# A prefill-and-decode step: selected branch and prompt attention in one block, key and value rings laid out anew, sliding values loaded earlier

## The chip, the cores and the metric

The kernel runs on one core of one Trainium2 chip, in fp32 throughout. The metric is the device time of one launch in microseconds. All times below are counted from the start of the profiled span.

## The reference, cut to what matters

One layer of a hybrid decoder for one prompt of 1024 tokens and 8 samples of 4 new tokens each (8192 tokens of past). The part that matters here is mixer B of the samples, native sparse attention, and what follows it, the attention of the prompt:

```python
# samples, per (sample b, token t, KV head g); 4 query heads r share a KV head
p_slc   = sum over r of softmax(q . kc + bias)         # compressed branch, 128 blocks
top_i   = top 16 blocks of 64 tokens                   # first, current and previous block forced
o_slc   = softmax(q . K[blocks] + bias) @ V[blocks]    # paged cache_slc_k / cache_slc_v
o_win   = softmax(q . Kwin + bias) @ Vwin              # cache_win_k / cache_win_v, 512 + 4 keys
o_b     = g0 * o_cmp + g1 * o_slc + g2 * o_win
# mixer A: dilated attention, window groups (128,1), (512,4), (2048,16), for samples and prompt
# prompt: dilated (A), selected (all started blocks) and sliding branch, 1024 x 1024, causal
x = x + concat(o_a, o_b) @ w_out;  ConvFFN;  final norm
```

In the kernel the selected branch of a sample is computed over all 8192 keys, with a penalty added to the keys of blocks that were not chosen, so the whole key and value cache of that branch is read: 8 samples x 4 chunks, each chunk 128 x 2048 floats (1.05 MB), for keys and again for values, 64 gathers in all.

## The kernel before, in words

The program is a row of blocks; in a block each engine has its own instruction list, written by hand, and engines meet only at semaphores. Leaving a block, and clearing a stage's semaphores (`Mem.end`, L60), makes all engines wait for each other. The stages, with where they lie in the profiled span:

- `front` (input projection, compression) and `compressed_and_dilated` (L1222 ff.), one shared block, to about 620 us. In its last part PE works through the dilated window of the samples in 16 items (`Selected.turns`, `load_item`), each of about 1.8 MB, in 7 slots of 4096 columns of the large tile `space`. Keys of the second four samples are transposed until 593 us, then the values of that group are multiplied (`values(1)`, L1533) until 616.5 us, which gives `d_pv` its second count. SP loads the sliding keys (`cache_win_k`, two DMAs of 1 MB) as soon as the last keys are transposed, and then stores the compressed part of the prompt's mix in eight pieces of 256 KB (`scr_mixc`, L1454, semaphore `s_mixc`). POOL issues the first four key gathers (`gather_keys`) at 594 to 599 us.
- `sample_selected` (L1894 ff.), its own block, about 620 to 817 us. A ring of six half slots holds key chunks (`key(i)` is half slot 4 + i) and another six hold value chunks (`value(i)`: half slots 0 to 3, then 10 and 11). Half slots 8 and 9 first hold the sliding keys, and 10 and 11 the sliding values, which SP loads as the first thing of this block (L2041). PE: `window_keys` (L2111), `new_scores`, `window_scores`, then for each sample b and chunk c `keys(b,c)` (16 transposes of 128x128, L2175) and one chunk later `scores` (L2186); at (0,2) `window_probs`, at (0,3) `window_values` (L2164), which waits for the sliding values; for b >= 1 at c = 2 `probs(b-1)` (L2196), at c = 3 `values(b-1)` (L2214). PSUM has three banks for transposes; a bank is free when ACT or DVE has copied it (`by_act` says which of the two). DVE does both sliding softmaxes (L2352 to L2359) at (0,0), after its copies of chunk (0,0) and before those of (0,1). `scores(0,0)` waits until both are done with the score banks (`s_wl` 4). DVE's first `logits(0,0)` (L2370) waits for all eight `mixc` stores, because its buffer lies where they are read from.
- POOL issues all gathers of the stage. A key gather n waits until chunk n - 6 has been transposed. A value gather n waits from n = 4 on for `window_values` and from n = 6 on until PE has multiplied the values of sample (n - 6) // 4. They stand in one list, so what waits holds up all behind it.
- After the merge of the three branches (`merge`, L2225 to L2238, and DVE L2440 to L2448) comes `prompt_attention` (L909 ff.) in a block of its own, about 820 to 1164 us: 96 units of 128 queries, each with scores into PSUM (L1012), bias and maximum by DVE (L1167), exponentials by ACT (L1139), transposes (L1033) and values (L1053). The first item's operands are loaded during the stage before; POOL reverses the order of its queries at the start of the block (L1083, L1084).
- `ffn` (output projection, ConvFFN), to the end.

The DMAs that SP issues form one queue (q1 in the profile), those of POOL another (q0), and both use the same 16 DMA engines.

## Time and profile before

| what | us |
|---|---|
| three runs | 2131.23, 2125.96, 2129.39; median 2129.39 |
| the profiled execution, its own time | 2128.97 |
| its span, first to last instruction | 2126.8 |
| PE busy | 2033.3 (96%), granted clock 0.987 |
| DVE, ACT, POOL busy | 1116.7, 524.2, 571.3 |

The page divides the span in 40 slices of 53 us, each digit the busy share in tenths:

```profile
PE   6999999999878987999999999999999999999998
...
PEclk8999999999998999999999999999999999999999
DMA  8467677663796995232252315555666522601100
```

A 9 means nine tenths or more. Slices 11 to 15 (585 to 850 us by the place in the row, counting from 0) are those in which PE is below nine tenths and the DMA engines above it: these are the end of the dilated stage, the selected stage and the start of the prompt.

### The profile page before, as it was taken

What the parts mean: (1) busy time and instruction counts of PE and PEld (TensorE: products, weight loads), DVE (VectorE), ACT (ScalarE), POOL (GpSimd) and SP (SyncE); (2) the same over time, 40 slices, a digit from 0 to 9 for tenths busy, and PEclk for the clock granted to TensorE, in tenths of its full rate; (3) what the DMA queues carried; (4) which work ended last, traced back from release to release, by engine and by line L of the source; (5) the groups of instructions that cost most, each with busy time, mean ns of one, the idle gap of its engine ahead of it and who ended that gap; (6) DMA issues with size and microseconds to landing.
All of it is one profiled execution on the core that took longest, in us unless ns stands there. A gap on an engine that the chain in (4) does not pass through costs nothing. (4 is left out here: it accounts for less than half of the span.)

```text
span 2126.8 us, 31772 instructions
## 1 busy us (share of the span) xinstructions
PE 2033.3 (96%) x12334; PEld 1330.5 (63%) x12334; DVE 1116.7 (53%) x2518; ACT 524.2 (25%) x1146; POOL 571.3 (27%) x746
## 2 busy tenths in 40 slices
PE   6999999999878987999999999999999999999998
PEld 3445466665555665666676447888888888644443
DVE  4034455411534555766676456777777755611452
ACT  4111010001323444766766011011111111000001
POOL 0443234202033641112223241332223222303110
PEclk8999999999998999999999999999999999999999
DMA  8467677663796995232252315555666522601100
GB/s 218 140 214 278 256 285 279 240 213 115 258 381 248 420 418 180 100 90 60 69 157 58 118 59 198 198 198 198 212 224 219 178 80 61 238 4 30 42 40 40
DMA packets 156392, 373.04 MB, mean 175 GB/s; under 512 B 36981, under 2 KB 95085, under 8 KB 138189
## 3 DMA queue, kind: packets, MB, share of 16 engines
q1 hardware_dynamic: 126420, 149.63, 22.2%
q0 software_dynamic: 25280, 149.44, 18.1%
q10 hardware_dynamic: 4544, 71.95, 9.6%
q8 instruction: 99, 1.62, 0.3%
q14 instruction: 49, 0.40, 0.1%
HBM read 343.68 MB, written 98.60 MB: 208 GB/s over the span
## 5 line engine op out<-in xcount | busy, mean ns | idle before, releaser
L2899 PE MATMUL ff_ps<-ff_hx,whole_aw 128*128 128x264 f32 x2464 | 550.5, 386 | 0.9 <-DVE ff_hx L3278 0.9
L2899 PEld LDWEIGHTS ff_ps<-ff_hx,whole_aw 128*128 128x128 f32 x2464 | 467.1, 190 | 80.8 <-issue 1.4
L805 DVE STREAM_TRANSPOSE whole_space<-whole_space 128x512 f32<-128x512 f32 x256 | 155.3, 674 | 153.4 <-PE joint_bank L614 153.4
L578 PE MATMUL joint_bank<-in_w,in_xT 128*128 128x512 f32 (+1 forms) x512 | 201.5, 547 | 0.0
L1167 DVE CUSTOM_DVE_ANT_0 pa_L<-pa_psS,whole_space 128x512 f32<-128x512 f32 (+3 forms) x288 | 141.1, 532 | 46.6 <-PE pa_psS L1012 45.6
L1139 ACT ACTIVATE pa_L<-pa_L,pa_nm 128x640 f32<-128x640 f32 (+3 forms) x192 | 142.0, 741 | 51.3 <-DVE pa_nm L1179 51.2
L578 PEld LDWEIGHTS joint_bank<-in_w,in_xT 128*128 128x128 f32 x512 | 95.0, 190 | 94.2 <-issue 87.6
L2925 PE MATMUL ff_ps<-ff_hx,whole_space 128*128 128x512 f32 x336 | 148.0, 593 | 0.0
L703 ACT ACTIVATE in_yout<-joint_bank 128x128 f32<-128x128 f32 (+5 forms) x88 | 41.0, 479 | 378.8 <-PE joint_bank L578 200.0
L3359 DVE SCALAR_TENSOR_TENSOR whole_space<-whole_space,ff_kept 128x1024 f32<-128x1024 f32 x88 | 124.4, 1414 | 3.1
L614 PE MATMUL joint_bank<-whole_space 128*64 128x256 f32 (+1 forms) x1152 | 121.6, 364 | 0.0
L1033 PE MATMUL pa_psT<-whole_ident,pa_L 128*128 128x128 f32 x816 | 112.9, 281 | 8.4 <-ACT pa_PT L1133 8.4
L1012 PE MATMUL pa_psS<-whole_space,pa_qT 64*128 64x512 f32 (+3 forms) x576 | 115.6, 507 | 5.5 <-POOL pa_qT L1083 5.5
L1033 PEld LDWEIGHTS pa_psT<-whole_ident,pa_L 128*128 128x128 f32 x816 | 87.2, 141 | 48.9 <-ACT pa_L L1139 17.9
L592 PE MATMUL joint_bank<-in_xT,in_w 128*128 128x352 f32 x384 | 117.6, 463 | 0.0
L3140 ACT ACTIVATE whole_space<-whole_space 128x1056 f32<-128x1056 f32 x22 | 23.8, 1083 | 368.5 <-DVE whole_space L3361 368.5
L2925 PEld LDWEIGHTS ff_ps<-ff_hx,whole_space 128*128 128x128 f32 x336 | 63.6, 190 | 80.6 <-issue 80.6
L1053 PE MATMUL pa_psO<-pa_PT,whole_space 128*64 128x128 f32 x1632 | 110.3, 279 | 0.9 <-DVE pa_tmp L1209 0.5
L1133 ACT ACTIVATE pa_PT<-pa_psT 128x512 f32<-128x512 f32 (+2 forms) x182 | 91.5, 538 | 56.2 <-PE pa_psT L1033 55.2
L614 PEld LDWEIGHTS joint_bank<-whole_space 128*64 128x64 f32 x1152 | 74.8, 137 | 47.2 <-issue 13.0
L2800 PE MATMUL ff_ps<-whole_space 128*128 128x512 f32 x224 | 97.7, 593 | 1.7 <-issue 1.7
L592 PEld LDWEIGHTS joint_bank<-in_xT,in_w 128*128 128x128 f32 x384 | 71.8, 190 | 42.3 <-issue 3.9
(435 smaller groups left out, 2647.8 us busy)
## 6 DMA issues: line engine op xcount, KB each, us to landing
out_new_a_k_s<-in_cache_a_k ACTq DMA_DIRECT2D x8, 4088.0 KB
out_new_a_v_s<-in_cache_a_v ACTq DMA_DIRECT2D x8, 4088.0 KB
whole_aw<-in_w_up SPq DMA_DIRECT2D x44, 512.0 KB, 7.6
in_w<-in_w_in SPq DMA_DIRECT2D x5, 2048.0 KB, 13.3
whole_space<-in_cache_a_k SPq DMA_DIRECT2D x8, 1024.0 KB
whole_space<-in_cache_a_v SPq DMA_DIRECT2D x8, 1024.0 KB
ff_hx<-in_w_down SPq DMA_DIRECT2D x14, 512.0 KB, 4.3
whole_space<-in_x_prompt SPq DMA_DIRECT2D x12, 512.0 KB, 9.2
```

Of the source, the lines that this page charges most:

```text
L578: mm = pe.matmul(ps[0:n, b, 0:width], xT[:, k, t * P:t * P + n], w[:, at % WBUF, k, 0:width], start=(k == 0), stop=(k == KC - 1))
L592: mm = pe.matmul(ps[:, b, 0:n], w[:, at % WBUF, k, c * P:c * P + P], xT[:, k, r0:r0 + n], start=(k == 0), stop=(k == KC - 1))
L614: mm = pe.matmul(psH[dh * HD:dh * HD + HD, r % 2, o0:o0 + n], w1[:, kv, t16, dh, :], rows[:, dh, t, :], start=(t16 == 0), stop=(t16 == 15) ...
L805: last = dve.transpose(put[:, dh, :, k * HD:k * HD + HD].rearrange("p t (g b) -> p t g b", g=2), got[:, :, :, dh, :])
L1012: pe.matmul(psS[:, c % 2, h, 0:w], qT[r, i, qt * P:qt * P + P], kT[i][r, j0 * P + k0:j0 * P + k0 + w], start=True, stop=True).then_inc(s_q ...
L1033: mm = pe.transpose(psT[:, b % 3, (x - x0) * P:(x - x0) * P + P], turned, ident[:, :])
L1053: mm = pe.matmul(psO[h * HD:h * HD + HD, u % 2, 0:P], V[i][:, j0 + j, v0:v0 + HD], PT[:, u % 3, (2 * j + h) * P:(2 * j + h) * P + P], star ...
L1139: nc.scalar.activation(x, x, ACT.Exp, bias=nm[:, s, h:h + 1], scale=1.0, accum_out=sm[:, s, h:h + 1]).then_inc(s_ex, 1)
L1167: dve.tensor_tensor_reduce(L[:, u % 3, h, 512 * x:512 * x + n], psS[:, c % 2, h, 0:n], T[it % 2][:, h, SEQ - w + 512 * x:SEQ - w + 512 * x ...
L2899: mm = pe.matmul(ps[:, bank_of(x, j, g), 0:H2], aw[:, j % 2, at, k, :], hx[:, bt, k, g * H2:g * H2 + H2], start=(k == 0), stop=(k == KH - 1))
L2925: mm = pe.matmul(ps[:, b, :], a[:, k, :], wd(k0 + k)[:, c0:c0 + 512], start=(k == 0), stop=(k == KD - 1))
L3359: dve.scalar_tensor_tensor(out=out[:, 0:SEQ], in0=U[:, v, k:k + SEQ], scalar=tap(k), in1=out[:, 0:SEQ], op0=ALU.mult, op1=ALU.add)
```

## The change

It does the following.

1. `sample_selected` and `prompt_attention` share one block, one set of eight PSUM banks and one set of semaphores (`late`). Each engine goes from its last instruction of the one to its first of the other. In place of the barrier stand waits on `s_merged` (the merge's own step counter): PE's second unit waits for step 7, SP's loads for the prompt's second item for step 10. POOL reverses the first item's queries at the end of its list for the selected stage, into a place of their own (`q0`), in two halves. The merge's products move from score banks 0 and 1 to 2 and 3. DVE waits for one more store (`s_mixed` 16) before the merge's last steps.
2. Rings: `key(i)` is now half slot 4, 5, 10, 11, 8, 9 and `value(i)` 0, 1, 2, 3, 6, 7. Half slots 6 and 7 are free with the last dilated keys, so SP loads the sliding values right behind the sliding keys, in the dilated stage, ahead of the `mixc` stores. Half slots 10 and 11 are free only with the last dilated values, so of the first four key gathers the first two stay where they were and the other two wait for `d_pv` 2.
3. `by_act`: of chunk (0,1) ACT copies pieces 0, 1 and 2 and DVE piece 3; before it was the other way round. `scores(0,0)` waits for the first sliding softmax only (`s_wl` 2), and `scores(0,2)` for both.

The diff, cut to its core:

```diff
     def key(self, i):
-        return self.half(4 + i)
+        return self.half((4, 5, 10, 11, 8, 9)[i])
     def value(self, i):
-        return self.half(i if i < 4 else 6 + i)
+        return self.half((0, 1, 2, 3, 6, 7)[i])
+    def load_window(self, sp, name, at, sem):
+        for x in range(2):
+            sp.dma_start(at(4 + x).rearrange("p (b t) c -> p b t c", b=4),
+                         self.io[name][4 * x:4 * x + 4, :, :].rearrange("b (p t) c -> p b t c", t=4)).then_inc(sem, 16)
...
+        self.q0 = at(slot[1] + 3 * SEQ + 4 * NB * NT, SEQ)
...
# compressed_and_dilated, POOL
             pool.wait_ge(d_pv, 1)
-            for c in range(4):
+            for c in range(2):
+                pre.gather_keys(pool, 0, c)
+            pool.wait_ge(d_pv, 2)
+            for c in range(2, 4):
                 pre.gather_keys(pool, 0, c)
# compressed_and_dilated, SP
             sp.wait_ge(d_tr, use["keys", NB - 1, NTL - 1] + 1)
-            for x in range(2):
-                sp.dma_start(pre.key(4 + x)..., io["cache_win_k"]...).then_inc(pre.s_wk, 16)
+            pre.load_window(sp, "cache_win_k", pre.key, pre.s_wk)
+            pre.load_window(sp, "cache_win_v", pre.value, pre.s_wv)
             for n in range(QT):
# sample_selected
-        psT = m.ps("psT", [P, 3, 512])
-        psS = m.ps("psS", [P, 4, 512])
-        psV = m.ps("psV", [P, 4, P])
+        psT = bank[:, 0:3, :]
+        psS = bank[:, 4:8, :]
+        psV = bank[:, 3, :].rearrange("p (a n) -> p a n", a=4)
-        block = m.block()
...
             if kind == "keys":
-                return at[2] == 3 if at[1] == 1 else at[2] % 2 == 0
+                if at[1] == 1:
+                    return (at[2] == 3) == (at[0] > 0)
+                return at[2] % 2 == 0
...
         def _(sp):
-            for x in range(2):
-                sp.dma_start(pre.value(4 + x)..., io["cache_win_v"]...).then_inc(s_wv, 16)
# sample_selected, end of POOL's list
+            pool.wait_ge(ops.s_q0, 16)
+            half = SEQ // 2
+            for x in range(2):
+                pool.tensor_copy(ops.q0[:, x * half:x * half + half].rearrange("p (t n) -> p t n", n=P),
+                                 backwards(ops.qL[0][:, x * half:x * half + half], half // P)).then_inc(ops.s_qr, 1)
# sample_selected, PE
-                if n == 0:
-                    pe.wait_ge(s_wl, 4)
+                if n in (0, 2):
+                    pe.wait_ge(s_wl, n + 2)
# sample_selected, DVE's merge
             dve.wait_ge(s_fp, 2)
+            dve.wait_ge(ops.s_mixed, 16)
             for w in range(2):
-                r = dve.tensor_tensor(o1[:, w, :], psS[:, w, 0:NB * 32], GB[:, 1 + w, :], ALU.mult)
+                r = dve.tensor_tensor(o1[:, w, :], psS[:, 2 + w, 0:NB * 32], GB[:, 1 + w, :], ALU.mult)
# prompt_attention
+            sp.wait_ge(s_merged, 10)
             load(1)
...
+                        q = qT[r, i, qt * P:qt * P + P] if it else ops.q0[r, qt * P:qt * P + P]
...
                     if s == 1:
                         pe.wait_ge(s_qr, 2)
+                        pe.wait_ge(s_merged, 7)
...
-            pool.wait_ge(s_ld[0], 96)
-            pool.tensor_copy(qT[:, 0, 0:P]..., backwards(qL[0][:, 0:P])).then_inc(s_qr, 1)
-            pool.tensor_copy(qT[:, 0, P:SEQ]..., backwards(qL[0][:, P:SEQ], QT - 1)).then_inc(s_qr, 1)
```

## Rows read from the trace of the kernel before

**Rows 1.** The page: the chain that ended last, by line.

```profile
PE ff_ps L2899 25%; PE ff_ps L2925 11%; PE ff_ps L2978 2%; PE ff_ps L2800 1%; PE ff_ps L2935 0%; PE ff_ps L2909 0%; PE ff_ps L2867 0%; DVE ff_hx L3275 0%; DVE ff_hx L3277 0%; DVE ff_hx L3278 0%; DVE ff_hx L3266 0%; DVE ff_hx L3259 0%; PE ff_ps L2943 0%; ACT whole_space L3152 0%; DVE whole_space L3403 0%
```

**Rows 2.** Busy time by stretch: us (instructions), granted PE clock, DMA share, GB/s.

```profile
602.00:620.00 18.00, 12.48 (x270) 9.12 (x269) 2.63 (x7) 1.08 (x2) 0.00 (x0) 0.91 1.03 386
...
648.00:654.00 6.00, 0.27 (x8) 0.25 (x12) 0.74 (x4) 0.00 (x0) 0.00 (x0) 0.82 0.53 221
654.00:663.00 9.00, 9.00 (x104) 6.35 (x96) 1.98 (x4) 1.19 (x2) 3.14 (x3) 0.55 0.19 57
663.00:680.00 17.00, 16.20 (x230) 11.84 (x227) 9.67 (x22) 7.13 (x17) 3.23 (x4) 1.00 0.56 220
...
700.00:800.00 100.00, 88.29 (x1203) 63.12 (x1201) 54.72 (x115) 41.56 (x88) 55.85 (x54) 1.00 1.01 418
...
816.00:821.00 5.00, 0.05 (x2) 0.08 (x2) 1.20 (x4) 0.00 (x0) 0.48 (x2) 0.50 0.08 13
821.00:828.00 7.00, 7.00 (x30) 3.58 (x32) 4.19 (x20) 4.33 (x14) 1.26 (x3) 0.64 0.94 315
900.00:1000.00 100.00, 95.81 (x906) 67.40 (x902) 67.50 (x277) 69.42 (x161) 17.97 (x42) 1.00 0.26 72
```

**Rows 3.** Timeline of PE, 636 to 659: start, us, what, [idle before <- releaser].

```profile
636.42 1.12 PE L2175 MATMUL sb_psT<-whole_ident,whole_space 128*128 128x128 f32 x4 [4.33 <-DVE whole_space L2272]
637.47 1.93 PE L2186 MATMUL sb_psS<-whole_space,sample_Qb 128*32 128x512 f32 x8
639.33 3.08 PE L2175 MATMUL sb_psT<-whole_ident,whole_space 128*128 128x128 f32 x16
...
646.67 1.06 PE L2186 MATMUL sb_psS<-whole_space,sample_Qb 128*32 128x512 f32 x8
653.74 1.94 PE L2164 MATMUL sb_psV<-whole_space,sb_PTw 128*32 128x128 f32 x32 [6.00 <-DMA whole_space<-in_cache_win_v]
...
658.62 3.66 PE L2175 MATMUL sb_psT<-whole_ident,whole_space 128*128 128x128 f32 x16
```

**Rows 4.** Timeline of POOL: two value gathers that waited.

```profile
659.53 0.96 POOL L2069 DMA_INDIRECT whole_space<-in_cache_slc_v,sample_idx  x1 [14.05 <-PE sb_psV L2164]
...
680.11 0.95 POOL L2069 DMA_INDIRECT whole_space<-in_cache_slc_v,sample_idx  x1 [13.40 <-PE sb_psT L2175]
```

**Rows 5.** Timeline of PE, at 675.

```profile
675.28 3.68 PE L2214 MATMUL sb_psV<-whole_space,sb_PT 128*32 128x128 f32 x128
```

**Rows 6.** Timeline of SP's DMA issues; the first row is of 590 to 596.

```profile
593.19 1.73 SPq L1449 DMA_DIRECT2D whole_space<-in_cache_win_k  x2
595.96 9.70 SPq L1454 DMA_DIRECT2D scr_mixc<-cd_qp  x1
...
618.54 0.39 SPq L1458 DMA_DIRECT2D scr_mixT<-cd_mixA  x1
620.31 4.33 SPq L2041 DMA_DIRECT2D whole_space<-in_cache_win_v  x2
```

**Rows 7.** The gathers' DMA queue in 594 to 600: packets, MB, share of 16 engines.

```profile
q0 software_dynamic: 10, 0.08, 6.8%
```

**Rows 8.** The gathers' queue and SP's in 600 to 608.

```profile
q0 software_dynamic: 322, 2.38, 77.8%
q1 hardware_dynamic: 321, 0.64, 22.3%
```

**Rows 9.** SP's queue in 616 to 624.

```profile
q1 hardware_dynamic: 1871, 2.84, 99.0%
```

**Rows 10.** Timeline of all engines, 813 to 822.

```profile
813.44 1.97 PE L2238 MATMUL sb_psS<-sb_stackW,sample_vcs 128*128 128x32 f32 x16 [0.72 <-DVE sb_stackW L2436]
...
816.70 0.60 DVE L2448 TENSOR_TENSOR whole_space<-sample_mixB,sb_o 64x128 f32<-64x128 f32 x2
...
820.95 3.28 PE L1012 MATMUL pa_psS<-whole_space,pa_qT 64*128 64x128 f32 x12 [5.54 <-POOL pa_qT L1083]
...
821.90 0.29 DVE L1167 CUSTOM_DVE_ANT_0 pa_L<-pa_psS,whole_space 128x128 f32<-128x128 f32 x1 [4.60 <-PE pa_psS L1012]
```

More of the change, by code:

```diff
@@ L199, in __init__, with loaded @@
         self.s_mixc = m.sem("prompt_compressed_kept")
+        self.s_q0 = m.sem("first_queries_loaded")
+        self.s_qr = m.sem("queries_reversed")
+        self.q0 = at(slot[1] + 3 * SEQ + 4 * NB * NT, SEQ)
+    def loaded(self, it):
+        return self.s_ld[it % 2], 96 * (it // 2 + 1) - (0 if it % 2 else 16)
     def load_rows(self, sp, it):
@@ L906, in backwards, with prompt_attention @@
     return bass.AP(x.tensor, x.offset + step * (cols - 1), [[part, n], [step * cols, tiles], [-step, cols]])
-def prompt_attention(nc, io, scr, mixT, wo, cv, ident, ops, s_mix, s_wo, s_cvl):
+def prompt_attention(nc, io, scr, mixT, wo, cv, ident, ops, s_mix, s_wo, s_cvl, s_merged, late, bank, block):
     QT = SEQ // P
@@ L1889, in _, with sample_selected @@
                         dve.tensor_copy(outp[n], psX[:, 0, :]).then_inc(s_o[0], 1)
-def sample_selected(nc, io, scr, mixB, GB, Qb, idx, pre, ident, pen, OV, knew, s_nl, ops):
+def sample_selected(nc, io, scr, mixB, GB, Qb, idx, pre, ident, pen, OV, knew, s_nl, ops, late, bank, block):
     NQ = 4
@@ L1983, in sample_selected @@
         s_fp = m.sem("merge_step_by_pe")
-        block = m.block()
         use, on_act = {}, []
```

94 lines of the change are left out of this document (46 added, 48 removed).

## The prediction, made before the change was run

> **What bounds the kernel now.** I read the chain that ended last first, to know in which stages a saved microsecond comes through. As far back as it goes it is PE in the feed-forward part, matmul behind matmul [rows 1]; the prompt's attention before it has PE busy for 95.81 of 100 us and the DMA engines for a quarter (the row of 900) [rows 2]. Both are limited by their own PE work and load nothing that is tied to a point in time, so an earlier start of the prompt should reach the end whole. The question is when the prompt starts.
>
> The busy time by stretch then shows three kinds of time in the selected stage [rows 2]. In 700 to 800 the DMA engines are full (1.01, 418 GB/s): there the stage runs at the pace of its gathers. In 648 to 654 PE does 0.27 us of work in 6, and behind that hole the DMA engines are nearly empty too (0.19 in 654 to 663, 0.56 in 663 to 680). And in 816 to 821 PE and DMA both stand. The timelines say why. PE waits 4.33 us before 636.42 for copies by DVE, and 6.00 us before 653.74 for the sliding values [rows 3]. POOL's value gather of 659.53 waited for the product of those values (14.05 us), and that of 680.11 for the product of the first sample's values (13.40 us), which PE makes from 675.28 to 679.2 [rows 4, 5]. So the early PE holes empty the DMA queue, and from the gather of 680.11 on the queue stays full. The whole later stage hangs on when that gather goes out.
>
> **The change part by part.** I work against the profiled execution, 2128.97 us, 0.4 us under the median of the three runs.
>
> *Who copies chunk (0,1), and the split wait.* DVE copies the three pieces only after both sliding softmaxes, and PE stands 4.33 us for the first of them. With ACT copying pieces 0 to 2 (its list has nothing else there) PE transposes the fourth piece, computes `scores(0,0)`, which needs only the first softmax, and transposes half of chunk (0,2), until its bank waits for DVE's one copy, which ends about when PE goes on now, at 636.4. That is 1.12 + 1.93 + 1.54 (half of 3.08) = 4.6 us of work [rows 3] moved into the hole. DVE saves two copies, ACT takes two more. `scores(0,2)` then ends near 643.1 in place of 647.73 (646.67 + 1.06): gain **4.6**, between 3 and 5.
>
> *Sliding values loaded 25 us earlier.* Before, the issue stands at 620.31 and takes 4.33 us [rows 6]. After, it stands behind that of the sliding keys (593.19). The 6.00 us wait goes, if the values are there by 643, which the queue sums below give (about 619). Gain **6.0**. What is late next is not the keys of sample 1: their gathers (chunks 4 to 8) go out as before, in a queue of unchanged bytes.
>
> *PE's clock behind the hole.* In 654 to 663 PE is busy all the time at a granted clock of 0.55, close to the lower of its two levels (1.2 GHz), after it had stood still for 6 us; 16 transposes take 3.66 us there [rows 2, 3]. In the same 9 us at the full level I would expect up to 4 us less, and nothing less if the hole that remains (about 2 us at 634 to 636) is enough to hold it down. The nearest row is that of 663 to 680, with short holes and clock 1.00. I take **3**, range 0 to 4.
>
> *What these are worth later.* All three bring forward the first sample's value product, hence `s_pv` 1, hence the gather of 680.11, and the stream behind it is continuous to the end of the stage. I count them at full value: 13.6. The DMA engines have room for it: in 648 to 680 they carried 0.53 x 6 + 0.19 x 9 + 0.56 x 17 = 14.4 us worth of 32 [rows 2], so 17.6 us of them were empty, more than the shift.
>
> *The two key gathers that now wait.* Chunks 2 and 3 are issued at 616.5 and not at 597 and 598. PE wants chunk 2 at about 634, and neither was waited for before. POOL has nothing else there, and needs twice 0.96 us [rows 4] and a little between, so it reaches the barrier at about 618.8, with SP (618.54 + 0.39 [rows 6]). Cost 0.
>
> *SP's queue at the barrier.* Sliding values (two DMAs of 1.05 MB) now stand before the eight `mixc` stores, the new values and the store of `mixA`, and SP must have issued all of these before the barrier. The issue of the first store already took 9.70 us at 595.96, held up by a full queue [rows 6]. Two more issues cost 1.73 us if the queue takes them, as those of the sliding keys did [rows 6]; on the other hand, from about 607 SP's queue has the engines for itself, for want of gathers 2 and 3. The bounds are 0 (SP is held up by the queue anyhow, which now drains faster) and 3 (the held-up issues stand one behind the other). I take **+1**.
>
> *The mixc stores.* DVE's `logits(0,0)` waits for them. When both queues have work, SP's gets 0.64 MB in 8 us and the gathers' 2.38 [rows 8], so 0.08 against 0.30 MB per us; alone SP's moves 2.84 MB in 8 us, 0.355 per us [rows 9], and both together 0.386 (the row of 602) [rows 2]. Behind the item loads SP's queue must carry the block choice 0.5, sliding keys 2.1, sliding values 2.1 and mixc 2.1: 6.8 MB, of which 0.2 by 607, when gathers 0 and 1 (2.1 MB) are through. The next gathers are issued at 616.5 but move nothing for about 5 us, as those of 594.3 moved 0.08 MB before 600 [rows 7]. From 607 to 621 SP's queue moves 14 x 0.355 = 5.0 MB, or 5.4 at 0.386 (sliding keys and values are through by about 619). The 1.6 or 1.2 MB left take until 641 or 636 at 0.08 per us. DVE wants them at 637.4. I take a delay of **+2**, range 0 to 5. Before, SP's queue had the engines to itself there [rows 9], and the stores were in time.
>
> *One block.* Before, DVE ends the merge at 816.70 + 0.60 = 817.30 and does the first logits of the prompt at 821.90; PE ends its merge at 815.41 and starts the prompt at 820.95 [rows 10]. After, PE's first unit follows at 815.5 (the queries were reversed behind POOL's last gathers, the rest of the operands is loaded), its second within a us, after step 7 of the merge, and DVE goes on at 817.3: gain 821.90 - 817.30 = **4.6**. Also, the clock is 0.50 in 816 to 821, and 0.64 in 821 to 828 where PE is busy for 7.00 of 7 us [rows 2]. With no pause the start of the prompt should lose less: at most 7 x 0.36 = 2.5, at least nothing, because DVE sets the pace of the first small units. I take **1.0**. The second item's loads go out behind DVE's first logits and not just ahead of them, some 3 us later in this count; they are wanted eight units on. Cost 0. DVE's new wait for `mixA`'s store is for something issued at 618.54 [rows 6]; PE's second unit and all of DVE's prompt work are queued behind it. Cost 0. Reversing the queries, 1 us of POOL, is hidden behind the last value gathers. The semaphores of two stages are now cleared together after the prompt: between 0 and 0.5 us, taken as 0.
>
> *Sum:* -4.6 - 6.0 - 3.0 + 1.0 + 2.0 - 4.6 - 1.0 = **-16.2**, so 2128.97 - 16.2 = 2112.8, and with the 0.4 to the median **2113**. The best ends give -5 - 6 - 4 + 0 + 0 - 4.6 - 2.5 = -22.1 (2107), the worst -3 - 6 - 0 + 3 + 5 - 4.6 - 0 + 0.5 = -5.1 (2124).
>
> **The rivals.**
>
> *The gathers are the bound all along.* If the stage is bound by its bytes, early gains only fill the queue earlier and are given back. For it: 1.01 over 100 us [rows 2], and two thirds of the stage look like that. Against it: the 17.6 us of empty engines. It would leave the boundary alone: 2129.4 - 5.6 = 2123.8. The Trainium skill (DMA: Bandwidth & Descriptors, Rules for kernel authors) speaks for this one: spreading transfers over issuing engines gains no bandwidth, because all run on the same 16 engines. The full row of 700 agrees with it, the rows of 648 to 680 show that bandwidth was not what lacked there.
>
> *The boundary does not close.* PE or DVE meets another wait there (bank, queries, operands), and only the early gains stay: 2129.4 - 10.6 = 2118.8.
>
> *SP's queue starves.* This one ends on the other side. If SP's queue goes into 621 with 2.6 MB left and not 1.2 to 1.6, because the held-up issues left it empty for about 3 us, or the gathers start to move at 618 and not at 621, then at 0.08 MB per us the mixc stores land only when the gathers have run dry, at about 653 to 655. DVE stands at `logits(0,0)` for 18 us, with it the copies of chunk (0,2), PE and every gather behind. The time is 2129.4 - 10.6 + 3 + 18 - 5.6 = 2134.2, with no gain of clock. It costs more than everything else brings from 16 us of delay on, which is from a landing at about 653. For it: the 4 to 1 sharing [rows 8], the 9.70 us issue [rows 6]. Against it: a full megabyte would have to be missing from a sum of 6.8.
>
> **How the numbers follow.** The forecast as summed, 0.78; bound by bytes, 0.08; boundary does not close, 0.08; starved queue, 0.04; something else on either side of no change, 0.02. The predicted time is that of the forecast. The range is 2105 to 2123: the forecast's bounds without the outermost us at the upper end, with 2 us more at the lower one, for a clock that helps more than counted; the boundary rival lies in it. A measurement of this kernel can tell about 0.3%, 6.4 us. Faster: the forecast save its worst end and the boundary rival, 0.86. Same: bound by bytes (5.6 us) and the worst end of the forecast, 0.10. Slower: 0.04.
>
> **What would show it.** In the changed kernel: the wait of L2164 for the sliding values is gone and the product starts near 644; the 4.33 us hole is 2 us or less; the clock of the 9 us behind is near 1.00 (if it is still near 0.55, that term is wrong); the second stalled value gather goes out near 669 and the merge ends near 806; between DVE's last merge step and the prompt's first logits there is under 0.5 us; the block ends about 16 us before 1164. If SP reaches the barrier after 622, or DVE waits for `mixc` longer than 5 us at L2370, the queue sum is wrong. If the gather of 680.11 moves forward by 12 us and the merge by less than 5, the first rival holds. The prediction is wrong altogether if a stage behind 821 runs longer than before.

## The result, and the profile after

The changed kernel takes 2130.53 us in the median of 22 runs, against 2127.78 for the kernel before: a ratio of 1.0014, 95% interval 1.0009 to 1.002. The interval lies just above 1, so the kernel is slower by a hair, and within the 0.3% that the prediction takes as no change. 2113.0 was forecast, with a range of 2105 to 2123. The profiled execution of after spans 2128.8 us, that of before 2126.8.

Busy time by stretch of after (us, then PE, PEld, DVE, ACT, POOL busy, PE clock, DMA share, GB/s), to be held against [rows 2]:

```profile
620.00:632.00 12.00, 0.70 (x4) 0.67 (x5) 0.60 (x2) 0.00 (x0) 0.24 (x2) 0.50 0.88 345
648.00:654.00 6.00, 6.00 (x36) 3.97 (x37) 4.62 (x10) 1.71 (x3) 5.25 (x5) 0.72 0.98 381
654.00:663.00 9.00, 8.54 (x129) 5.68 (x128) 5.63 (x16) 2.58 (x6) 3.67 (x4) 1.00 0.73 279
700.00:800.00 100.00, 89.43 (x1195) 62.84 (x1194) 53.94 (x117) 41.74 (x91) 56.11 (x55) 0.98 1.02 416
816.00:821.00 5.00, 5.00 (x22) 2.31 (x22) 2.87 (x13) 3.33 (x11) 0.59 (x2) 0.65 0.89 277
900.00:1000.00 100.00, 96.86 (x934) 68.39 (x932) 65.57 (x269) 68.03 (x162) 18.35 (x43) 1.00 0.26 73
1155.60:1162.80 7.20, 0.01 (x1) 0.02 (x1) 0.43 (x2) 0.00 (x0) 0.61 (x2) 0.63 0.00 0
1162.80:1175.50 12.70, 12.69 (x81) 5.13 (x81) 2.05 (x4) 1.20 (x2) 4.79 (x4) 0.63 0.90 328
```

The holes that the change was aimed at are gone: PE is busy for all of 648 to 654 (0.27 us before), the 9 us behind run at clock 1.00 (0.55 before), and 816 to 821 is full. But two stretches in which PE does nothing are new: 620 to 632, and 1155.6 to 1162.8.

The first one, in PE's timeline of after (start, us, what, [idle before <- releaser]), which answers to [rows 3]:

```profile
631.30 0.39 PE L2120 MATMUL late_bank<-whole_ident,sample_knew 32*128 32x32 f32 x2 [14.34 <-PEq L70]
...
647.22 1.37 PE L2190 MATMUL late_bank<-whole_ident,whole_space 128*128 128x128 f32 x8 [1.72 <-DVE whole_space L2287]
...
655.23 1.06 PE L2179 MATMUL late_bank<-whole_space,sb_PTw 128*32 128x128 f32 x32
...
657.93 2.00 PE L2190 MATMUL late_bank<-whole_ident,whole_space 128*128 128x128 f32 x16
```

The hole of 4.33 us is now 1.72, the product of the sliding values waits for nothing, and 16 transposes take 2.00 us where they took 3.66. All of it lies behind a pause of 14.34 us at the barrier (the sequencer, PEq, at L70). SP's issues and POOL's timeline, which answer to [rows 6] and [rows 4], say what held the barrier:

```profile
594.82 13.35 SPq L143 DMA_DIRECT2D whole_space<-in_cache_win_v  x2
608.21 9.06 SPq L1466 DMA_DIRECT2D scr_mixc<-cd_qp  x6
...
624.67 0.49 SPq L1470 DMA_DIRECT2D scr_mixT<-cd_mixA  x1
```

```profile
616.27 0.94 POOL L149 DMA_INDIRECT whole_space<-in_cache_slc_k,sample_idx  x1 [19.25 <-PE joint_bank L1545]
617.51 0.94 POOL L149 DMA_INDIRECT whole_space<-in_cache_slc_k,sample_idx  x1 [0.30 <-issue]
631.11 0.12 POOL L2092 MEMSET sb_Ln<- 128x32 f32 x1 [12.66 <-POOLq L70]
...
677.76 0.96 POOL L2079 DMA_INDIRECT whole_space<-in_cache_slc_v,sample_idx  x1 [11.76 <-PE late_bank L2190]
```

SP was through at 625.2 and not at 618.9, 6.2 us later. POOL (GpSimd) had issued its last gather by 618.45 and then stood for 12.66 us. The raw records of the trace name it: a DRAIN of GpSimd, an instruction with which the block ends. It lasts until 629.88; the last gathers landed at 624.6 and 627.7. The page counts no drain as work, it shows only as idle time "<-POOLq".

The boundary to the prompt closed as forecast [rows 10], and then the end of the merged block opened. DVE's first logits of after; the first FFN work of after on POOL and PE; and PE's of before:

```profile
814.14 0.29 DVE L1177 CUSTOM_DVE_ANT_0 pa_L<-late_bank,whole_space 128x128 f32<-128x128 f32 x1
```

```profile
1162.64 1.27 POOL L3050 TENSOR_TENSOR whole_space<-whole_space 128x512 f32<-128x512 f32 x1 [6.17 <-POOLq L70]
...
1162.81 1.08 PE L2804 MATMUL ff_ps<-whole_space 128*32 128x512 f32 x4 [7.20 <-PEq L70]
```

```profile
1164.68 0.64 PE L2787 MATMUL ff_ps<-whole_space 128*32 128x512 f32 x4 [1.90 <-PEq L70]
```

Again GpSimd's drain: 5.48 us from 1155.99, where before it took 0.56. The two spans come apart as follows (differences of start times in the two traces, us):

| stretch | before | after | change | forecast |
|---|---|---|---|---|
| start to POOL's first work behind the barrier | 620.31 | 631.11 | +10.80 | +1 |
| from there to the second stalled value gather | 59.80 | 46.65 | -13.15 | -13.6, +2 for mixc |
| from there to the end of the merge on DVE | 137.19 | 136.34 | -0.85 | 0 |
| boundary to the prompt's first logits | 4.60 | 0.04 | -4.56 | -4.6 |
| prompt attention, to PE's last product | 340.88 | 341.47 | +0.59 | -1.0 |
| gap before the FFN | 1.90 | 7.20 | +5.30 | 0 |
| FFN up to its first long group of products | 9.86 | 12.67 | +2.81 | 0 |
| that group (224 products) and all behind it | 952.26 | 953.32 | +1.06 | 0 |
| sum | 2126.8 | 2128.8 | +2.0 | -16.2 |

The second row counts from a barrier that stands 10.8 us later in after, and transfers went on in that time (the sliding values landed at 624.4, ahead of it). It shows that the waits behind the barrier are gone, and not what each change would be worth with the barrier in its old place.

### The profile page after: what moved, and what is told of

It is laid out like the page before. It is cut to its first block and busy times, and to the rows that moved or that the text cites. A ratio compares the mean times of both kernels' runs of the same rounds, so it can differ in the third digit from the quotient of the medians.

```text
span 2128.8 us, 31737 instructions
## 1 busy us (share of the span) xinstructions
PE 2035.3 (96%) x12334; PEld 1328.0 (62%) x12334; DVE 1105.1 (52%) x2516; ACT 525.4 (25%) x1148; POOL 577.0 (27%) x746
## 5 line engine op out<-in xcount | busy, mean ns | idle before, releaser
L1177 DVE CUSTOM_DVE_ANT_0 pa_L<-late_bank,whole_space 128x512 f32<-128x512 f32 (+3 forms) x288 | 141.1, 531 | 42.2 <-PE late_bank L1025 41.7
L1046 PE MATMUL late_bank<-whole_ident,pa_L 128*128 128x128 f32 x816 | 113.2, 281 | 8.5 <-ACT pa_PT L1143 8.5
L1046 PEld LDWEIGHTS late_bank<-whole_ident,pa_L 128*128 128x128 f32 x816 | 87.4, 141 | 49.7 <-ACT pa_L L1149 18.4
L1066 PE MATMUL late_bank<-pa_PT,whole_space 128*64 128x128 f32 x1632 | 110.3, 278 | 0.9 <-DVE pa_tmp L1219 0.5
L1143 ACT ACTIVATE pa_PT<-late_bank 128x512 f32<-128x512 f32 (+2 forms) x182 | 91.6, 539 | 56.7 <-PE late_bank L1046 55.3
L1025 PE MATMUL late_bank<-whole_space,pa_qT 64*128 64x512 f32 (+3 forms) x528 | 104.0, 498 | 0.0
```

Source lines behind the costliest of these rows:

```text
L1046: mm = pe.transpose(psT[:, b % 3, (x - x0) * P:(x - x0) * P + P], turned, ident[:, :])
L1066: mm = pe.matmul(psO[h * HD:h * HD + HD, u % 2, 0:P], V[i][:, j0 + j, v0:v0 + HD], PT[:, u % 3, (2 * j + h) * P:(2 * j + h) * P + P], star ...
L1177: dve.tensor_tensor_reduce(L[:, u % 3, h, 512 * x:512 * x + n], psS[:, c % 2, h, 0:n], T[it % 2][:, h, SEQ - w + 512 * x:SEQ - w + 512 * x ...
```

## The experiments

Two theories were set against each other first: that the two drains and what SP has queued took the gain back, or that the gain was never there (the gathers as the bound, the rings, the semaphores cleared together). Then each term of the sum was priced alone. Each median is of that kernel's runs, each ratio is to the kernel before on the same chip, with its 95% interval. The runs were made on several chips, on which the median of the kernel before lay between 2127.15 and 2129.18, so a difference between the medians of two rows is good to some 2 us; the ratios allow for the chip.

| run | base and edit | us | ratio |
|---|---|---|---|
| late_nodrain | after, merged block ends without the drain | 2121.15 | 0.9972 (0.9961 to 0.9983) |
| joint_nodrain | after, dilated block ends without it | 2125.37 | 0.9992 (0.9982 to 1.0002) |
| both_nodrain | both | 2118.31 | 0.9957 (0.9941 to 0.9972) |
| gathers_behind_barrier | after, key gathers 2, 3 behind the barrier | 2121.10 | 0.9963 (0.9949 to 0.9977) |
| behind_barrier_late_nodrain | that and late_nodrain | 2112.30 | 0.9937 (0.992 to 0.9955) |
| best_values_behind_barrier | that, sliding values behind the barrier | 2110.72 | 0.9928 (0.9907 to 0.9949) |
| best_unsplit | 2112.30's kernel without the split | 2117.33 | 0.9952 (0.9936 to 0.9968) |
| best_unmerged | 2112.30's kernel without the merge | 2116.42 | 0.9958 (0.9944 to 0.9972) |
| no_merge | after without the merge | 2126.92 | 1.0000 (0.9986 to 1.0013) |
| rings_alone | before with rings, early values, late gathers | 2130.79 | 1.0007 (0.9997 to 1.0017) |
| split_alone | before with the split | 2128.02 | 0.9999 (0.9989 to 1.0008) |
| before_gathers_behind | before, key gathers 2, 3 behind the barrier | 2118.69 | 0.9951 (0.9938 to 0.9964) |
| before_gathers_split | that and the split | 2115.15 | 0.9950 (0.9919 to 0.9981) |
| before_small_dma | before, one software DMA in the prompt's block | 2128.08 | 1.0008 (0.9995 to 1.0022) |

Three more have a single run each, for a drain's length: drain_in_the_middle, before_40_gathers, before_40_plain. The merge alone, on before's rings, was not measured: with a tile of its own for the reversed queries (merge_alone) the kernel's tiles do not fit into SBUF. So the merge is priced only on top of the rings.

### The drains

**late_nodrain.** GpSimd's drain at the end of the merged block is left out. Nothing here needs it for its data, as each gather is waited for by its reader.

```diff
-            block = late.block()
+            block = late.block(no_gpsimd_drain=True)
```

> After, with the merged block closed without GpSimd's drain. Theory (drains laid bare): in after the gap between the last product of prompt attention and the first of the FFN is 7.20 us (1155.61 to 1162.81), 5.48 of it GpSimd's drain, and the two groups of 32 products behind it take 6.02 us where before had 3.64. Without the drain the gap is 1.6 to 2.0 us, the groups take 3.6 to 4.2, and the time is 6 to 8 us under after's, 2122.5 to 2124.5. Rival (the merge costs by its semaphores): more are cleared at one place, so the gap stays at 6 us or more and the time within 1 us of after's. Rival (the gap is cover): output weights or FFN weights that load in it are late next, so the gap closes but the first products of the FFN wait as long, and the time falls by less than 2.

Measured: 2121.15, 9.4 us under after's median (8.9 by the ratios). The gap and the first products behind it:

```profile
1158.62 5.34 PE L2804 MATMUL ff_ps<-whole_space 128*32 128x512 f32 x32 [2.04 <-PEq L70]
```

The gap is 2.04 us, as expected, and the rival of the semaphores falls: the same are cleared at the same place (0.44 us in both). The 32 products still take 5.34 us, not 3.6 to 4.2; but from the first of them to the first long group it is 9.94 us (before 9.86, after 12.67). The long group itself takes 107.06 us (after 108.49, before 107.58). So the exposed drain cost 5.2 us itself, 2.7 by a colder start behind it (after's clock is 0.63 from 1155.6 through 1175.5, and 0.83 in late_nodrain over the same products) and up to 1.4 in the long group: 9.3 in these stretches. The two spans differ by 8.4, since PE came to the gap 1.0 us later here (1156.58 against 1155.61). My 6 to 8 left the last part out.

**joint_nodrain** and **both_nodrain.** The same edit to the block that ends in the dilated stage, and to both.

```diff
-                block = joint.block()
+                block = joint.block(no_gpsimd_drain=True)
```

> After, with the block that ends in the dilated stage closed without GpSimd's drain. Theory: there the drain waits for the two late key gathers (landed at 624.6 and 627.7, drain over at 629.88) while SP is free at 625.2; without it the barrier follows SP, at 626.2 to 626.8 instead of 631.11, and the 4.5 us stay to the end: 2125.5 to 2126.5. Rival (SP's queue alone holds the barrier): barrier at 631, time as after's 2130.5. Rival (the gathers bound the stage): the barrier comes earlier, but the value gathers still queue behind the same bytes, the window values product or the second stalled value gather starts where it did (655.2 and 677.8), and the time falls by under 1.5 us.

> After, with both blocks closed without GpSimd's drain. Theory: the two gains add, 10 to 12.5 us under after's 2130.5: 2118 to 2120.5, that is 7 to 10 us under before. Rivals: if either drain is cover for something else, the sum is short by that part (2123 to 2126).

Measured: 2125.37 and 2118.31, 5.2 and 12.2 us under after. In joint_nodrain the barrier follows SP, whose last issue came later than in after (626.14, not 624.67):

```profile
626.14 0.48 SPq L1470 DMA_DIRECT2D scr_mixT<-cd_mixA  x1
```

```profile
628.28 0.39 PE L2120 MATMUL late_bank<-whole_ident,sample_knew 32*128 32x32 f32 x2 [11.08 <-PEq L70]
```

The second stalled value gather moves with it, from 677.76 to 673.84, 3.9 us for 3.0 at the barrier: the stage is not held by its bytes. Without the drain the block does not wait for what is in flight: in both_nodrain PE starts behind the barrier at 624.73, and the last gather lands at 625.65. The theory of the drain holds, but it is half of the story, since PE still stands for 11.08 us.

And the first block's drain, left out, is not paid later. The drain at the end of joint_nodrain's merged block takes 5.47 us, as after's, though 294 software DMAs (DMAs that GpSimd issues) had gone out since the last one, and not 60. On POOL:

```profile
1161.19 2.50 POOL L3050 TENSOR_TENSOR whole_space<-whole_space 128x512 f32<-128x512 f32 x2 [6.18 <-POOLq L70]
```

**gathers_behind_barrier.** Both drains stay; key gathers 2 and 3 become POOL's first work behind the barrier.

```diff
             for c in range(2):
                 pre.gather_keys(pool, 0, c)
-            pool.wait_ge(d_pv, 2)
-            for c in range(2, 4):
-                pre.gather_keys(pool, 0, c)
...
+            for c in range(2, 4):
+                pre.gather_keys(pool, 0, c)
             pool.memset(Ln[:, :, :], NEG).then_inc(s_z, 1)
```

> After, with key gathers 2 and 3 issued first thing behind the barrier instead of ahead of it; both drains stay. Theory (the drain waits for gathers in flight): GpSimd's drain is over with gathers 0 and 1, by 613, the barrier follows SP at 624 to 627, and of the 4.5 to 6 us some 0 to 3 are lost to keys that land 10 us later: 2126 to 2129. Rival (SP's queue alone): the barrier stays at 629 or later and the time is after's or above, 2130.5 to 2133.

Measured: 2121.10, 9.4 us under after (10.9 by the ratios) and well below the 2126 to 2129 expected. SP and PE:

```profile
618.53 1.16 SPq L1467 DMA_DIRECT2D scr_mixT<-cd_mixA  x1
```

```profile
621.26 0.39 PE L2119 MATMUL late_bank<-whole_ident,sample_knew 32*128 32x32 f32 x2 [5.34 <-PEq L70]
```

Not only the drain is early (over by 609.58): SP's last issue ends at 619.7 and not at 625.2. I had taken SP's queue for delayed by the sliding values alone. The two gathers' bytes, the last of which landed at 627.7 in after, most often hold it up as well: in the seven profiles that have them ahead of the barrier together with the early sliding values, SP is through at 623.1 to 626.6 in six and at 617.2 in one (rings_alone); in the four that have only the early values there, at 617.9 to 619.7 in three and at 624.1 in one (best_unsplit). What makes the two exceptions is not shown. And nobody waits for the keys that come later: the second stalled value gather goes out 45.6 us behind the barrier's first PE work (46.5 in after). With the merged block's drain left out too (behind_barrier_late_nodrain, 2112 to 2116 expected) the time is 2112.30: the two losses add.

**drain_in_the_middle.** After with `pool.drain()` behind POOL's reversal of the first queries, where nobody waits for POOL.

> After, with one more drain of GpSimd behind its reversal of the first queries, while the other engines merge the branches; the drains at the blocks' ends stay. Theory (what the drain at the end clears is left by the software DMAs since the last drain, once): the added drain takes some 5 us where nothing waits for GpSimd, the one at the end under 0.8 instead of 5.48, the gap before the FFN is about 2 us, and the one look is some 5 to 8 us under after's. Rival (a drain at the end of a block with gathers has a fixed price): the last drain takes 5 us again and the time is after's.

One run: 2122.65. The added drain ran from 798.42 for 11.45 us, hidden, the one at the end of the block took 0.56, and the gap was 2.29 us:

```profile
1159.10 5.34 PE L2805 MATMUL ff_ps<-whole_space 128*32 128x512 f32 x32 [2.29 <-PEq L70]
```

So within a block a drain clears once what the software DMAs since the last one left. The added one was longer than the 5 us expected as it began ahead of the last landing (807.4).

**before_small_dma**, **before_40_gathers**, **before_40_plain.** What does the length go by? One plain software DMA at the start of the prompt's block, and 40 of either kind, one in each of its first 40 units, of 16 bytes a row:

```diff
             for s in range(U + 4):
+                if s < 40:
+                    pool.wait_ge(s_probe, 16 * s)
+                    pool.dma_start(probe[:, :], io["c_flip"][:, 0:4]).then_inc(s_probe, 16)
```

> Before, with one small software DMA (128 x 4 numbers) issued by GpSimd at the start of the block of prompt attention, landed some 300 us before the block ends; nothing else is changed. Theory (a block in which GpSimd has issued any software DMA pays a fixed drain): the drain at the end of the block grows from 0.56 us to about 5.5, the gap before the FFN from 1.90 to about 7, and with the colder clock behind it the time rises by 6 to 7.5 us, to 2134 to 2135.5. Rival (the drain costs by the number of software DMAs or their bytes, 36 gathers and more in after): the drain stays under 1.5 us and the time within 1.5 us of before's.

> Before, with 40 tiny gathers (indirect software DMAs, 128 rows of 16 bytes) issued by GpSimd in the block of prompt attention, one in each of its first 40 units. Theory (each gather leaves something that the next drain clears, 5.48 us for after's 60, 0.09 each): the drain at the end of the block takes 3 to 4.5 us where one plain software DMA left 0.66. Rival (bytes or large rows set it): under 1 us. The issues themselves may lengthen the units; only the drain is read here.

> Before, with 40 tiny plain software DMAs (128 x 4 numbers) issued by GpSimd in the block of prompt attention, one in each of its first 40 units, where before_40_gathers had gathers. Theory (every software DMA since the last drain leaves some 0.08 us for the next): the drain at the end of the block takes 3.5 to 4.6 us, as with 40 gathers (3.83). Rival (gathers alone leave something): under 1 us.

My theory of a fixed price fell with the first: its drain took 0.66 us and the time is before's. With 40 it took 3.83 us for gathers and 3.84 for plain ones. The issues themselves lengthened the units, to 2164.39 and 2144.78 in all. The drains of GpSimd at the ends of blocks, from the raw records:

| drain | software DMAs since the last drain | last landing | starts | lasts |
|---|---|---|---|---|
| before, prompt | 0 | | 1163.16 | 0.56 |
| before_small_dma, prompt | 1 | long before | 1163.57 | 0.66 |
| before_40_gathers, prompt | 40 | long before | 1194.75 | 3.83 |
| before_40_plain, prompt | 40 | long before | 1172.54 | 3.84 |
| after, merged block | 60 | 807.5 | 1155.99 | 5.48 |
| gathers_behind_barrier, merged block | 62 | long before | 1146.61 | 5.64 |
| joint_nodrain, merged block | 294 (60 of them in the block) | long before | 1154.53 | 5.47 |
| after and before, FFN | 0 | | 2044.01, 2042.15 | 3.28 |
| late_nodrain, both_nodrain, FFN | 60, 294 (none in the block) | long before | 2035.65, 2029.68 | 3.28 |
| before, selected | 60 | 810.4 | 801.41 | 11.44 |
| before, dilated | 234 | 616.3 | 595.80 | 22.66 |
| after, dilated | 234 | 627.7 | 616.61 | 13.27 |
| gathers_behind_barrier, dilated | 232 | 607.5 | 593.81 | 15.77 |

A drain's record opens before GpSimd's last instruction ahead of it is done, and its length holds what that one still needs. At the end of the prompt that is an addition of 0.45 us, over 0.07 us before the drain's end in before (1163.65 and 1163.72), and in the FFN one of 3.17 us, also over 0.07 before the end. In the rows of the dilated and the selected stage GpSimd's last gathers are still issued in it, in before's dilated one until 599.10 and in after's until 618.45. So the drain's own share of the 0.56 and of the 3.28 is near nothing.

Where all had landed, 0, 1, 40, 60 and 62 fit 0.56 us and 0.082 us for each: (3.84 - 0.56) / 40, and (5.48 - 0.56) / 60. Kind and size don't matter. Only those of the same block count: 234 of an earlier block add nothing in joint_nodrain (5.47 for 5.48), and 60 or 294 of earlier blocks add nothing to the FFN's 3.28. What takes them off where a block ends without the drain is not shown. Where some are still in flight, the drain ends 2.1 to 2.5 us behind the last landing. The price per DMA isn't shown beyond 62: 234 times 0.082 would be 19.2 us, and after's took 13.27.

### The terms of the sum, one by one

**no_merge** and **best_unmerged.** After without the merge, and the same with the gathers behind the barrier.

> After without the merge: before with the rings, the sliding values, the two late key gathers and the split of the first copies. Against after it tells what the merge is worth. Theory (4.6 us won at the boundary of prompt attention, 5.3 lost to the drain at the end of the merged block, up to 2 to a colder clock behind it): 1 to 3 us under after's 2130.5, so 2127.5 to 2129.5, with the barrier near 629 to 631 and a gap of 1.9 before the FFN. Rival (the merge is a gain, as the prediction had it): 4 us and more above after's, 2134.5 or later.

> The gathers behind the barrier, but no merge: no_merge with key gathers 2 and 3 behind the barrier; all drains are there, hidden behind the merge of branches or short. Against 2112.3 it prices the merge without its drain. Theory: the boundary is worth 4.6 us, so 2116 to 2118. Rival (most of the merge's gain was lost elsewhere in the prompt stage too, as after's 4.56 at the boundary but no more later): under 2114.

Measured: 2126.92 and 2116.42. With its drain in the open the merge costs 3.6 us (2130.53 - 2126.92; 3.0 by the ratios). Without that drain it gives 4.1 (2116.42 - 2112.30; 4.5 by the ratios). The intervals of the two ratios overlap in both cases. no_merge has the late barrier (PE starts at 631.19) and the short gap:

```profile
1163.01 3.64 PE L2794 MATMUL ff_ps<-whole_space 128*32 128x512 f32 x32 [1.89 <-PEq L70]
```

**split_alone** and **best_unsplit.** The split of the first copies alone in before, and taken out of the kernel of 2112.30.

```diff
-                return at[2] == 3 if at[1] == 1 else at[2] % 2 == 0
+                if at[1] == 1:
+                    return (at[2] == 3) == (at[0] > 0)
+                return at[2] % 2 == 0
...
-                if n == 0:
-                    pe.wait_ge(s_wl, 4)
+                if n in (0, 2):
+                    pe.wait_ge(s_wl, n + 2)
```

> The split of the first copies alone (which engine copies chunk 1 of sequence 0, and the wait in two steps) in before. Theory (the wait for the sliding values stands behind it): the hole of 4.33 us shrinks, and the products for the sliding values wait as much longer, since the values land at 653.7 all the same: 2127 to 2128.5, nothing gained. Rival (the prediction's terms add one by one): 4.6 us and part of the clock, 2120.5 to 2123.5.

> The fastest kernel so far (2112.3) with the first copies split as in before. It prices the hole of 4.33 us where nothing stands behind it. Theory (the prediction's terms of 4.6 and a part of the clock's 3.0): 2116 to 2119, with a hole of about 4 us back between 640 and 650. Rival (the products wait for keys there in any case, as these come later now): 2111 to 2113.5.

Alone it gives nothing, 2128.02. PE in split_alone:

```profile
636.42 1.38 PE L2177 MATMUL sb_psT<-whole_ident,whole_space 128*128 128x128 f32 x8 [0.85 <-DVE whole_space L2274]
...
654.34 1.93 PE L2166 MATMUL sb_psV<-whole_space,sb_PTw 128*32 128x128 f32 x32 [10.63 <-DMA whole_space<-in_cache_win_v]
```

The hole of 4.33 is 0.85, and the wait of 6.00 for the sliding values is 10.63: what one gave, the next wait took. Where no such wait stands behind it, the medians put the split at 5.0 us (2117.33 - 2112.30) and the ratios at 3.2, with intervals that overlap. The hole in best_unsplit and in the kernel of 2112.30:

```profile
641.62 0.82 PE L2187 MATMUL late_bank<-whole_ident,whole_space 128*128 128x128 f32 x4 [3.30 <-DVE whole_space L2284]
```

```profile
635.41 1.37 PE L2189 MATMUL late_bank<-whole_ident,whole_space 128*128 128x128 f32 x8 [1.05 <-DVE whole_space L2286]
```

Counted from the first PE work behind the barrier, as the profile of best_unsplit has a late barrier (625.66 against 619.46), the prompt's scores start 185.7 us later there and 181.2 in the other: 4.6. The same count, to the prompt's first logits, gives 3.3 for rings_alone and no_merge (191.83 and 188.49) and 2.7 for before_gathers_behind and before_gathers_split (193.04 and 190.33). So 3 to 5 us.

**rings_alone.** Before with the new rings, the early sliding values and the two late key gathers.

> The rings alone: before, with after's rings, sliding values and two late key gathers; no merge, and the first copies split as in before. Theory: the barrier slips by some 10 us as in after (GpSimd's drain behind the late gathers, SP's queue behind the sliding values), the wait for sliding values (6.0) goes and the hole of 4.33 stays: 3 to 5 us slower than before, 2131 to 2133, and a gap of 1.9 before the FFN. Rival (prediction: queues cost 3 at most): 2122 to 2125.

Measured: 2130.79, not told from before's time, at the lower edge of what the theory gave. SP's last issue, and PE:

```profile
616.27 0.93 SPq L1465 DMA_DIRECT2D scr_mixT<-cd_mixA  x1
```

```profile
630.27 0.39 PE L2109 MATMUL sb_psT<-whole_ident,sample_knew 32*128 32x32 f32 x2 [14.52 <-PEq L70]
```

Here SP is done at 617.2 and the barrier still comes 13 us later, by the drain alone.

**best_values_behind_barrier.** The sliding values go back behind the barrier in the kernel of 2112.30. Then **before_gathers_behind** and **before_gathers_split**: before, with no more than key gathers 2 and 3 moved behind the barrier, and with the split beside it.

```diff
-            for c in range(4):
+            for c in range(2):
                 pre.gather_keys(pool, 0, c)
...
+            for c in range(2, 4):
+                pre.gather_keys(pool, 0, c)
             pool.memset(Ln[:, :, :], NEG).then_inc(s_z, 1)
```

> The fastest kernel so far (gathers behind the barrier, no drain at the end of the merged block, 2112.3) with the sliding values loaded behind the barrier again, as before has them. It prices the early load where no drain hides it. Theory (the prediction's term of 6.0 holds): the values land at 645 to 652 instead of ahead of 630, the products wait 5 to 7 us at about 650, and the time is 2116.5 to 2120. Rival (the early load only moves bytes, since the key and value gathers then come sooner): 2111 to 2113.5.

> Before, with key gathers 2 and 3 moved from ahead of the barrier to the first place behind it; nothing else. Theory (the gathers, in large packets, hold up what SP has queued: the stores ahead of the barrier and the sliding values behind it): the barrier comes no later than 619, the sliding values land before 645 instead of at 653.7, their wait of 6.0 us goes, and the hole of 4.33 stays: 2119 to 2122.5. Rival (keys that come later are waited for, and the early load of the sliding values is what removes their wait): 2126 or more.

> The same with the first copies split as in after; still before's rings, no early load, no merge. Theory (the rings and the early load are worth nothing): as best_unmerged, which differs by them alone, 2115 to 2117.5. Rival (they are worth the prediction's 6.0): 2121 or more.

My first theory fell: 2110.72, and no wait for the sliding values, though they are issued at 618.61. The early load is worth nothing once the gathers are out of the way (the 1.6 us between the two medians are within their intervals). The second held: the two gathers alone, moved in before, give 2118.69, 9 us by the medians and 10 by the ratio, more than any term of the forecast, and a third of a us under the 2119 to 2122.5 expected. PE's hole stays, its wait for the sliding values is gone, as they land at 644.4 and not at 653.7:

```profile
636.29 1.11 PE L2177 MATMUL sb_psT<-whole_ident,whole_space 128*128 128x128 f32 x4 [4.44 <-DVE whole_space L2274]
```

The DMA queues in 600 to 612 show what changed (packets, MB, share of 16 engines), first before, then before_gathers_behind:

```profile
q0 software_dynamic: 473, 3.49, 76.7%
q1 hardware_dynamic: 471, 0.92, 21.6%
```

```profile
q1 hardware_dynamic: 869, 1.73, 47.8%
q0 software_dynamic: 288, 2.10, 51.8%
```

The gathers' 8 KB packets had left SP's 2 KB packets 0.92 MB in 12 us; with two gathers fewer SP moves 1.73. Its sliding keys and mixc stores are out of the way earlier, and the sliding values find a free queue: their two issues take 1.44 us together, not 4.33 [rows 6]. In before both queues move nearly the same number of packets while both have work, 473 and 471 here and 322 and 321 in [rows 8], so the one with 7.4 KB a packet (3.49 MB in 473) takes 3.8 times the bytes of the one with 2.0. The Trainium skill (DMA: Bandwidth & Descriptors, Queues, rings and completion order) says that each DMA engine takes turns between its queues packet by packet. Its packet is a group of typically 9 to 17 descriptors; the equal counts agree with such turns, but that its packets are the ones the profile counts is not shown. before_gathers_split comes out at 2115.15 (2115 to 2117.5 expected); the split's 3.5 us between these medians is not told from nothing by the ratios (0.9951 and 0.9950), and best_unmerged, which adds the rings and the early values, is no faster (2116.42).

## Why the prediction was wrong, point by point

**What bounds the kernel: right.** An earlier start of the prompt comes through to the FFN whole (-7.76 at the first logits, -7.17 at PE's last product of prompt attention), and the stream of gathers shifts with the gather of 680.11. The rival that the gathers are the bound is refuted by joint_nodrain. One loose statement ahead of the rows, on which no term rests: of the slices 11 to 15 the DMA engines are at nine tenths in 11, 13 and 14 alone, and PE is at nine tenths in 13.

**Who copies chunk (0,1): mechanism right, size about right.** 4.6 was taken; the hole fell from 4.33 to 1.72, and the split is worth 3 to 5 where nothing hides it. But it stood first in a chain of two waits, and alone it gives 0 (split_alone).

**Sliding values early: the wait went, the cause was wrong.** I took the wait of 6.00 for a matter of the issue time. It was one of the queue: the gathers ahead of the barrier held up what SP had to move. My own rows had it [rows 8], and I used them only for mixc. The values landed at 624.4 and not at about 619, in time all the same.

**PE's clock behind the hole: the clock right, its price not measured alone.** Clock 1.00 in place of 0.55, and 16 transposes in 2.00 us and not 3.66. With the two above, 13.15 of 13.6 us came, counted from the late barrier.

**The two key gathers later, cost 0: wrong, this is the step that failed.** I let POOL reach the barrier with the end of its last issue, at 618.8. It reached it at 629.9, since the drain waits for the landing (627.7) and 2.2 us more. The last gather's issue row of 0.94 us ends at 618.45, and the landing comes 9.3 us behind it. The Trainium skill (Perfetto Trace Analysis, DMA Instruction — SWDGE (GPSIMD)) says that such an instruction ends in the profile when its descriptors are made and not when the data has moved, and the landing times here agree. In before there was a drain too, over at 618.46 (last landing 616.3), half a us ahead of SP's 618.93, which hid it. What is hidden in the trace of before is not free when the work ahead of it moves by 19 us. The barrier came 10.8 us later and not 1, and with the two gathers behind it the kernel takes 9.4 us less.

**SP's queue at the barrier: +1, range 0 to 3, wrong.** It measured +6.2. In after the drain hides it, and with the drain left out the barrier follows it (joint_nodrain). Half of the premise failed: SP's queue did not have the engines for itself, as the bytes of the moved gathers came into it until 627.7. With them gone SP's last issue is over at 619.7. That the sliding values stand ahead costs little as a rule and 5 us in one profile (PE's first work behind the barrier, with the gathers behind it: 619.46, 620.07, 621.26 and 625.66 with them, 618.80, 620.33 and 621.85 without).

**The mixc stores: +2 did not come.** With the barrier at 631 they were in time (landed at 632.1, and DVE comes to its logits at 647.1), and with the gathers behind it also (624.4 and 635.3 in the kernel of 2112.30).

**One block: the boundary right (4.56 for 4.6), the drain missing, the second step that failed.** The merge took away the block end at which POOL's drain of 60 gathers was hidden (801.41 to 812.85, within the merge of branches), and put it where everyone waits: 5.48 us, and 2.8 more in a colder FFN start. I had priced the semaphores cleared together (0 to 0.5; 0.44 against 0.13 us), and not the drain beside them, which I put at nothing. The clock's 1.0 at the prompt's start did not come either: prompt attention took 0.59 us more, though 816 to 821 is full now, at clock 0.65.

**The rivals.** None was the one that came. The slower one (SP's queue starves, 2134.2) named the right queue, with the wrong waiter. The one that was missing: the barrier waits for what POOL has in flight.

**The sum.** -16.2 was forecast and +2.0 came, 18.2 us apart. The barrier is 9.8 of them (10.80 for 1), the gap and the cold start before the FFN 8.1 (5.30 and 2.81 for nothing); the rest, within 1.6 us a row, nearly cancels.

With both losses taken away the kernel runs at 2112.30 and 2110.72, beside the 2113 forecast. That is partly luck: of the terms, the early values' 6.0 is worth nothing in these kernels, and the gathers moved behind the barrier, which were no term, stand in its place.

## What to carry to other kernels

The end of a block makes GpSimd wait for the software DMAs in flight, and costs 0.08 us here for each that it issued in the block. Before moving a gather toward a block's end, or merging a block full of gathers with one behind it, look up in the records where the drain lies and what hides it; a drain set where GpSimd is idle, or left out where every reader waits for its data, brings the time back, and the one left out was not paid at the next block's end. A transfer that lands 25 us before its use should be looked at for what it delays: two gathers in large packets, moved behind a barrier, were worth 9 us here, more than the three changes aimed at visible waits gave on top of it (6.4 by the medians, 2118.69 to 2112.30, and 3.0 by the ratios, with the merged block's drain left out).

And terms that stand one behind the other on one chain are not a sum until each is shown alone: the hole's 4.6 us were worth 0 by themselves in before.

## What the runs showed of the hardware

GpSimd's drain at the end of a block is over 0.07 us behind GpSimd's last instruction where the block issued no software DMA, and takes 0.082 us more for each that it issued, plain or gather, small or 1 MB, with all landed long ago (1, 40, 60 and 62 of them); with gathers in flight it ends 2.1 to 2.5 us behind the last landing. Those of an earlier block that ended without its drain add nothing (5.47 us with 294 since the last drain, 60 of them in the block). The page counts none of it as busy: it shows as "<-POOLq" on POOL and "<-PEq" on PE. Behind a pause of 7.20 us, PE took 12.67 us to the first long group of the FFN; behind one of 2.04 us it took 9.94, and behind 1.90 us 9.86. Its clock in these products was 0.63 in the first case (after) and 0.83 in the other two (late_nodrain, before).
